# Sharing the down-projection weight blocks of the first two token tiles, and a new order of work ahead of the third

## The reference

```python
x = x + 0.5 * swiglu(rms_norm(x, ffn1_norm[l]), ffn1_w_gate[l], ffn1_w_up[l], ffn1_w_down[l])   # width 2816
h = rms_norm(x, mix_norm[l]); proj = h @ w_in[l]          # 512 q | 128 k | 128 v | 512 u
out_a = sliding_window_sink_attention(rope(q), rope(k), v, sinks)   # window 128, 8 heads on 2 kv heads
out_b = multiscale_pool(u, pool_w[l], pool_scale[l])      # trailing means of 2, 4, 8, 16, minus the token, then a matrix
x = x + concat(rms_norm(out_a), rms_norm(out_b)) @ w_out[l]
x = x + memory_cross_attention(rms_norm(x), rms_norm(mem), wq, wkv, wo)   # 256 memory rows, 4 heads of 256
x = x + 0.5 * swiglu(rms_norm(x, ffn2_norm[l]), ffn2_w_gate[l], ffn2_w_up[l], ffn2_w_down[l])
```

## Time and profile before

| | |
|---|---|
| median of 3 runs | 5272.42 us (5269.86 to 5276.35) |
| profiled execution | 5268.95 us |
| span of its slowest core (core 6) | 5267.4 us |
| spans of the eight cores | 5243.3 to 5267.4 us |
| TensorE busy | 5029.0 us (95% of the span) |
| DVE, ACT, POOL busy | 2318.6, 1672.8, 996.2 us |
| share of the chain that ended last | PE 86%, DMA 7%, ACT 2%, issue 2% |

### The profile page before, as it was taken

The page is one execution under the profiler, slowest core; times in us unless marked ns, Lnnn a source line. Parts: engine busy times, 40 slices in busy tenths (PEclk is TensorE's granted clock), DMA queues, the critical chain, the costliest instruction groups (busy, mean ns, idle before and its releaser), DMA issues.

```text
span 5267.4 us, 79366 instructions; the slowest of 8 cores (5243.3 to 5267.4 us)
## 1 busy us (share of the span) xinstructions
PE 5029.0 (95%) x25501; PEld 2481.0 (47%) x25872; DVE 2318.6 (44%) x3808; ACT 1672.8 (32%) x2840; POOL 996.2 (19%) x1106
## 2 busy tenths in 40 slices
PE   7869989999999999999999999999999999999998
PEld 3433434444444454555545444444444445455555
DVE  3133545354453534353526254454535344445353
ACT  2225343223333332233323232232323223233342
POOL 1121221121212112121211121212221121212111
PEclk9989999999999999999999999999999999999999
DMA  7877777666576687888655445454454545555654
GB/s 160 178 178 192 192 188 217 200 177 205 178 194 192 184 228 197 230 232 241 211 179 192 164 152 180 156 170 155 158 166 140 180 151 193 164 202 192 200 168 164
DMA packets 259936, 974.53 MB, mean 185 GB/s; under 512 B 31104, under 2 KB 33280, under 8 KB 257696
## 3 DMA queue, kind: packets, MB, share of 16 engines
q1 hardware_dynamic: 220608, 793.12, 46.4%
q0 software_dynamic: 37776, 174.22, 15.8%
q10 hardware_dynamic: 1152, 2.10, 0.1%
HBM read 986.48 MB, written 134.87 MB: 213 GB/s over the span
## 4 chain that ended last, share of the span: by engine, by line
PE 86%; DMA 7%; ACT 2%; issue 2%; DVE 2%; POOL 1%; SPq 0%; ACTq 0%; DVEq 0%; POOLq 0%
PE ps L355 86%; DMA sb_fr<-wfb 2%; DMA wab<-sb_mr 2%; DMA sb_fr<-wf 1%; DMA sb_x<-xT 1%; DMA sb_mr<-wxb 1%; ACT L148 1%; ACT sb_tmp L151 0%; DMA wfb<-sb_fr 0%; ACT sb_pT L151 0%; POOL sb_ach L462 0%; DVE sb_hF L490 0%; SPq L161 0%; DMA sb_ao<-memT 0%; DVE sb_hM L490 0%
## 5 line engine op out<-in xcount | busy, mean ns | idle before, releaser
L355 PE MATMUL ps<-sb_hF,sb_fr 128*128 128x512 bf16 (+1 forms) x12142 | 2532.8, 363 | 55.4 <-DMA sb_fr<-wfb 15.6
L355 PEld LDWEIGHTS ps<-sb_hF,sb_fr 128*128 128x128 bf16 x12320 | 1207.7, 98 | 1289.4 <-issue 90.8
L355 PE MATMUL ps<-sb_act,sb_fr 128*128 128x512 bf16 (+1 forms) x6062 | 1272.7, 362 | 39.5 <-DMA sb_fr<-wf 19.4
L572 DVE TENSOR_TENSOR sb_act<-ps,sb_sg 128x512 bf16<-128x512 f32 (+1 forms) x770 | 492.1, 642 | 1258.3 <-PE ps L355 963.3
L462 POOL TENSOR_TENSOR sb_acc<-sb_acc,sb_sqf 128x512 f32<-128x512 f32 (+2 forms) x516 | 613.2, 1189 | 2230.3 <-ACT sb_sqf L151 2227.0
L355 PEld LDWEIGHTS ps<-sb_act,sb_fr 128*128 128x128 bf16 x6160 | 599.6, 98 | 667.5 <-issue 70.8
L355 PE MATMUL ps<-sb_hM,sb_mr 128*128 128x512 bf16 (+1 forms) x3545 | 776.1, 363 | 46.1 <-DMA sb_mr<-wm 29.3
L151 ACT ACTIVATE sb_sg<-ps 128x512 f32<-128x512 f32 (+1 forms) x792 | 438.8, 559 | 1060.6 <-PE ps L355 917.7
L151 ACT ACTIVATE sb_sqf<-sb_x 128x512 f32<-128x512 f32 (+1 forms) x546 | 321.7, 591 | 998.6 <-DVE sb_x L913 435.1
L355 PEld LDWEIGHTS ps<-sb_hM,sb_mr 128*128 128x128 bf16 x3600 | 352.7, 98 | 413.3 <-issue 59.1
L151 ACT ACTIVATE sb_pT<-ps 128x512 bf16<-128x512 f32 (+2 forms) x436 | 233.7, 567 | 389.3 <-PE ps L355 382.4
(11 more groups left out here) (105 smaller groups left out, 2431.0 us busy)
## 6 DMA issues: line engine op xcount, KB each, us to landing
sb_fr<-wfb SPq DMA_DIRECT2D x1100, 512.0 KB, 4.5
sb_mr<-wmb SPq DMA_DIRECT2D x153, 512.0 KB, 4.6
sb_mr<-wab SPq DMA_DIRECT2D x144, 512.0 KB, 4.5
wfb<-wf POOLq DMA_DIRECT2D x74, 512.0 KB, 8.4
sb_fr<-wf POOLq DMA_DIRECT2D x66, 512.0 KB, 10.1
wfb<-sb_fr SPq DMA_DIRECT2D x58, 512.0 KB, 10.2
x<-sb_x POOLq DMA_DIRECT2D x24, 512.0 KB, 6.6
sb_x<-x POOLq DMA_DIRECT2D x24, 512.0 KB, 9.0
```

Source lines behind the costliest of these rows:

```text
L355: P.op("pe", lambda h: h.matmul(out_ap, lt, rh, start=st, stop=sp_, skip_group_check=True), reads=list(rb), writes=(ob_,), signal=(i == n ...
L572: P.op("dve", lambda h: h.tensor_tensor(out=a_, in0=d[1][0][:, :T], in1=sg[si][:, :T], op=ALU.mult), (d[1][1], sgb[si]), (ab_,))
```

## The change

It has seven parts. `f_dn` can share blocks between two callers, and the 8 chunks of dn0 and dn1 now alternate, so that the 11 down blocks are loaded once. The look-ahead of ring F stays 3 to the end of the first stage. A folded value block is stored by one DMA where there were four, and `advance` issues ring M's next loads right behind it. Each piece of tile 2's x waits only for the four a2b chunks that lie under it. The fourth memory unit moves ahead of dn1's last chunk (r), the loads of x of tile 2 come behind r, and then the mixer's projections k, u, v, q0 and q1. The trailing sums and the pooling matrices (wn, late) and q2 and q3 move into tile 2's first five gate groups. The attention of tile 0 has the next ten gate groups, its norm the next two, and the output projection the last five.

```diff
@@ load_x
-                ex = tuple(a2b) if v == 2 else ()
+                ex = tuple(a2b[4 * j:4 * j + 4]) if v == 2 else ()
                 P.dma("pool", xs[s][:, cs, :T], src[:, cs, c0:c0 + T], reads=rd, writes=tuple(xbs[s][cs]) + ex, box=xbox[s][j])
@@ f_dn
-        def f_dn(ti, l, f, key, act=act_main):
+        def f_dn(ti, l, f, key, act=act_main, shared=None):
...
-                            st["slot"] = load("F", "wf", l * 2 + f - 1, 22 + s)
+                            if shared is not None and s in shared:
+                                st["slot"] = shared[s]
+                            else:
+                                st["slot"] = load("F", "wf", l * 2 + f - 1, 22 + s)
+                                if shared is not None:
+                                    shared[s] = st["slot"]
@@ memkv_unit, b_part
-                    for s in range(4):
-                        P.dma("pool", dv[:, s, h, :], sv[:, s, :], reads=(ob_,), writes=(wabuf[l][4 + h],), box=abbox[d["o"]])
+                    P.dma("pool", dv[:, :, h, :], sv, reads=(ob_,), writes=(wabuf[l][4 + h],), box=abbox[d["o"]])
+                    advance("M", AHEAD["M"])
@@ v == -1
-                AHEAD["F"] += 1
...
-                dn0 = f_dn(0, 0, 1, ("mix", 0, 0))
-                dn1 = f_dn(1, 0, 1, ("mix", 1, 0), act=act_second)
-                run(sprinkle(merge(fl + dn0 + dn1[:12], kv0), [late_consts] + raw(ropes) + raw(rope_table_steps(1, 0))))
+                shared = {}
+                dn0 = f_dn(0, 0, 1, ("mix", 0, 0), shared=shared)
+                dn1 = f_dn(1, 0, 1, ("mix", 1, 0), act=act_second, shared=shared)
+                for m in range(8):
+                    fl += dn0[3 * m:3 * m + 3] + dn1[3 * m:3 * m + 3]
+                run(sprinkle(merge(fl[:-9], kv0), [late_consts] + raw(ropes) + raw(rope_table_steps(1, 0))) + raw(fl[-9:-3]))
+                dn1 = dn1[21:]
+                AHEAD["F"] += 1
@@ v == 0
-                r = raw(dn1[12:])
+                r = raw(dn1)
+                qs = [seg1[23 + 5 * c:28 + 5 * c] for c in range(4)]
                 hs = raw(seg1[:4])
-                run(r[:2] + early[1:] + r[2:4] + hs[:2] + r[4:5] + hs[2:] + r[5:])
+                ks = raw(seg1[4:8])
+                us = [f for g in range(4) for f in raw(seg1[8 + 3 * g:10 + 3 * g])]
+                wn = [seg1[10 + 3 * g] for g in range(4)]
...
-                rest = seg1[4:]
-                fs = raw(load_x(2)) + early[:1] + raw(rest[:16])
-                u3 = memkv_unit(0, 3)
-                fs += sprinkle(raw(rest[16:19] + u3[:4]), nsq) + nmm[:1]
-                fs += raw(u3[4:6]) + nmm[1:] + raw(u3[6:]) + nh[:2]
-                fs += sprinkle(raw(rest[19:]), nh[2:])
-                fs += sprinkle(merge(gu[:36], seg2), pre_conv[:4])
-                cov = [f for f, w in gu[36:42] if w > 0]
-                evs = [f for f, w in gu[36:42] if w == 0]
+                u3 = raw(memkv_unit(0, 3))
+                fs = u3[:3] + early[1:] + u3[3:5] + hs[:2] + u3[5:] + r + raw(load_x(2)) + hs[2:] + early[:1]
+                fs += sprinkle(ks + us + raw(seg1[20:23]) + [f for c in range(2) for f in raw(qs[c][:1] + qs[c][2:4])], nsq) + nmm + nh
+                late = [f for c in range(2) for f in (qs[c][1], qs[c][4])]
+                fs += merge(gu[:15], wn + late + qs[2] + qs[3])
+                fs += sprinkle(merge(gu[15:45], seg2), pre_conv[:4])
+                cov = [f for f, w in gu[45:51] if w > 0]
+                evs = [f for f, w in gu[45:51] if w == 0]
                 fs += cov[:3] + seg2n[:1] + cov[3:] + seg2n[1:2] + evs[:1] + seg2n[2:] + evs[1:]
-                fs += merge(gu[42:], segw)
+                fs += merge(gu[51:], segw)
                 fs += sprinkle(tail_steps(dn, seg4, tail), pre_conv[4:])
```

## The result

The changed kernel takes 5222.88 us (median of 4 runs, 5214.65 to 5233.78) where the kernel before takes 5271.14 beside it (4 runs, 5268.29 to 5276.35): 48.3 us less, a ratio of 0.9909 (0.9886 to 0.9931). The prediction was 5229. Many executions in the experiments ran at a lower granted clock on one half of the chip (cores 0 to 3 or 4 to 7) or on both, so times there are taken over the halves whose four granted clocks are all 0.984 or more.

A forecast was written before the change was run, and what follows sets the result against it. TensorE's idle time and slow-clock restarts before 470 us, 93.2 us, were what the edits can touch. With 49.4 left the gain is 43.8 from 5268.95, plus 3.5 for the median: 5229 us, own range 5213 to 5243.

The forecast's parts named there:

- Gates and down-projections: Two stretches, before 205 us and 205 to 275 us: TensorE idle falls from 3.4 to 1 and 26.5 to 7 us.
- What made wf late: Down-projections: wf blocks came late behind POOL's four folded stores; sharing halves the pace of fresh blocks and removes 16.7 us.
- Cover for tile 2: Stretch 322 to 405 us, before tile 2's gates: 24 us idle left of 41.3, bounds 15 and 35.
- POOL's hold: Last memory unit: POOL stands 9 us until the folded store lands, with tile 2's x pieces behind it.
- t0: The end of dn0's last chunk, from which the prediction times its steps in the cover for tile 2.
- Tile 2's gates: Stretch 405 to 470 us: 3 us left for late wf blocks, 7 for waits on DVE and ACT.
- Three blocks are now in their slots early: Tile 2's gates: blocks loaded ahead leave 3 us of the 7.7 mostly lost to wf blocks, bounds 0 and 8.
- Clock: TensorE restarts at 1.2 GHz after standing still: about four of seven stay, 7 us for 12.
- After 470 us: Past 470 us little can be won; idle time there differing by more than 5 us would make the prediction wrong.
- the folded store holds everything: Rival, POOL's one folded store: takes 63 us, POOL stands 54 us longer, time 5285 us; chance 5%.
- All is hidden: Rival, before 470 us: nearly all terms at lower bounds, 24 us stay, gain 69, about 5203 us; chance 12%.
- The transfers set the pace: Rival, 205 to 433 us: the 16 engines get no faster, gain 20, about 5252 us; chance 18%.

The follow-up runs named there:

- the second profile of the changed kernel: The changed kernel run again unaltered, beside the kernel before on the same chip; 5208.2 us against 5257.9, ratio 0.9907.

## Why the prediction came out right, step by step

The time and the sign were right. The mechanism up to 470 us was right in its main steps: 38 us won early in the first pair of profiles, 41 with the second profile of the changed kernel, where the sum had 43.8. But the whole is 48 to 50, and what makes it up was not in the sum.

- *Gates and down-projections.* 0 idle us where 1 and 7 were left. The step that took the middle of 0 to 15 was too careful: the DMA share of 205 to 275 us was 0.88, not higher, and still nothing was late. Neither part gives this alone (11.4 us stay with the store, up to 6.3 with sharing).
- *What made wf late.* The prediction gave this both to POOL's store and to the blocks' pace, and that is what the two parts alone show. It did not see that sharing with the old store would give much of its gain back in the next stage.
- *Cover for tile 2.* 24 us were forecast. By its own steps: b waits 8.28 (5), an a-step 2.08 (0), the scaling of hM 1.6 (2), q0's block 0.92 (3), and 7.7 go to the squares and the scaling of hF (9.4), 20.6 together. POOL's hold was 6.95 us (9). The x pieces nevertheless went out 33 us after t0 (280.2), not 26, and the first gate group started at t0 + 54.5, not 50.5. The step behind this is b's landing: the load went out at t0 + 3, as forecast, but took 14.43 us and not 8, and b ended at t0 + 21 where t0 + 13 was forecast.
- *Tile 2's gates.* 7 us were put down to ACT and DVE, 3 to DMA. ACT made 20 table loads of 1283 ns from 362 to 430 us, as counted, but TensorE waited 2.3 us for pT there, and 5.8 for ACT and DVE together. The DMA term was the mis-sized one, 10.9 us for 3, in one wait. The step that failed is "Three blocks are now in their slots early": the block that came late is a later one, and the conversions, which the new order leaves beside fewer gate groups, were not priced at all. So one sign did not come: TensorE's longest wait was to stand ahead of tile 2's first gates, 8 to 14 us, ended by the scaling of hF. That wait is 2.58 us, and the longest is the 10.87 us for this block.
- *Clock.* Busy time multiplied by what the granted clock lacks of 1, summed over the stretches, is about 22 us before and 17 after, an estimate from the two sets of windows. The 5 us difference is the forecast one; the level of what stays is not.
- *After 470 us.* "If idle time past 470 us differs by more than 5 us" was named as what would make the prediction wrong, and it does: the rest is 6 to 16 us shorter by the two profiles of the changed kernel, and TensorE stands 103.1 and 99.2 us past 480 us where it stood 109.5 (means over the cores). The window of layer 1's four units, which use the same store, has more than all of it: 24.3 and 22.1 us where it was 34.7. The list of what the change touches had missed that `memkv_unit` serves both layers.

So the total is nearer than its parts. An early gain some 3 to 6 us smaller than forecast and a late one of 6 us or more that was left out offset each other. That they nearly cancel is luck.

Of the rivals, *the folded store holds everything* is out: the whole store landed in 7.7 us, not 63, and in 17 behind x. *All is hidden* is out: 38.6 us of idle time stand in the windows. *The transfers set the pace* is wrong for the time. It fits the place where the idle time is now: the share is 0.95 and 1.01 from 275 to 405 us, neither four x pieces at once nor a better cover for b gives more than some 3 us of time there, and taking four transfers out gives 8.

The Trainium skill ("ScalarE: Activation LUTs", What ACT_TABLE_LOAD costs) speaks of a drain of about 1380 ns at each switch of sets. No row of after shows it: the 10 gate activations (sb_sg) from 362 to 430 us, all but one of them right behind a load, waited 0.1 us together.

## What to carry to other kernels

A DMA issue that waits for the DMA before it is paid by every load queued behind it on that engine, so the stores of a unit are looked at before the traffic of its loads, and in every place that calls the same function. When a part wins time in one stage, follow the same queue into the next one before the gain is booked: here sharing alone won 20 us in its stretch and kept 7. Bulk transfers that no step needs soon belong where the DMA share is low; four of them moved out of a stretch at 1.01, into one that had 0.50 to 0.60 (433 to 520 us of after), gave 8 us.

## What was not expected of the hardware

A load of 512 KB on SP's queue, which takes a median of 6.0 us, took 28.95 us when four conversions of 512 KB from DRAM to DRAM had been issued within 2 us just ahead of it on POOL's; the conversions took 20.4 us. The Trainium skill ("DMA: Bandwidth & Descriptors", Issuing engines are not separate DMA queues) says that transfers of all issuers interleave on the same 16 engines, and these rows agree. And 512 KB stored as four quarters, each waiting for the one before, took POOL 25.4 us from the first issue to the last in one unit of the kernel before, and 13.0 and 17.2 in the two after it, where one store of the same bytes landed in 7.7 us, and in some 17 behind a tile of x.
